# A second group of cached keys from the turned layout in every step, and a head's loads moved to other slots

## The chip, the cores and the metric

One core of a Trainium2 chip. The metric is the device time of one execution in microseconds, the median of three runs. All arithmetic is float32.

## What is computed

Two layers of a decoder for 1024 prompt tokens and, beside them, 8 samples of 8 new tokens each. Layer 0 has a gated linear recurrence (HGRN2, 4 heads) and latent attention (MLA, 4 heads) side by side, layer 1 another recurrence; each is followed by an MLP. The change concerns layer 0, and there the attention of the 64 new tokens to their samples' caches, 64 pages of 128 rows each:

```
past = cache_mla[e][page_table].reshape(Bd, past_len, LAT_DIM)      # 8 x 8192 rows of 320
s = (einsum('bqhc,bkc->bhqk', q_lat, c_kv) + einsum('bqhr,bkr->bhqk', q_pe, k_pe)) * MLA_SCALE
p = softmax(where(k_pos <= q_pos, s, NEG_BIG))
out = einsum('bhqk,bkc->bqhc', p, c_kv)                             # c_kv: the first 256 of 320
```

The recurrence is evaluated in chunks, per head: with log decays summed along the tokens, the pairs within a chunk are formed level by level (distance 1, 2, 4 ... 64), each level a product of decayed queries and keys.

## The kernel before

The program is a row of stages with a barrier between them: load, even (layer 0's projections), latent, prompt attention, **mix**, even out, MLP, then layer 1. Stage mix (`even_mix_stage`) does the cached attention of the samples and, in its gaps, the recurrence of the 4 heads.

**Attention.** 512 pages are worked off in 32 steps of 16 pages; a step is 4 groups of 4 pages, and a sample is 4 steps. POOL fetches the rows of a group with one indirect DMA (`ask_for_rows`) into a ring of 12 slots, after the values of two steps before have been formed (`pool.wait_ge(valued, step)`). For the scores a key must lie turned, 128 features on the partitions. It comes so in one of two ways. Either PE transposes the rows it has (`turn_keys`, L2229), four 128x128 pieces to a unit, through the four PSUM banks KB, from which ACT or DVE copies each unit into `keys` (L2408, L2587: DVE takes units 1 and 3). Or SP loads the pages from a copy of the cache that the host has turned (`ask_for_keys`, L1660: for each page read its number from the table into a register, and issue a DMA of 160 KB). A group of the second kind needs only its 256 value columns from POOL (L1649) instead of all 320 (L1651). Group 3 (`M.COME`) is of the second kind in every step, with two buffers `kd`. Group 2 is so in the even steps from 2 on (`M.TWICE`), with one buffer `kd_more`; in the others it is transposed:

```
def units(step):
    return 5 if step in M.TWICE else 8
```

Units 0 to 4 are the keys of groups 0 and 1 (20 transposes), units 5 to 7 those of group 2 (10 transposes, and 512, 512 and 256 columns to copy, all by ACT).

**Order on PE.** Written out by hand. `score` waits for the copies of the step's keys and for both kinds of loaded keys (L2236, L2238).

```
for step in range(STEPS):
    score(step)
    slot(2 * step)
    turn_p(step - 1)                      # if step
    turn_keys(step + 1, 0), turn_keys(step + 1, 1)
    value(step - 1)                       # if step
    turn_keys(step + 1, 2 ...)
    slot(2 * step + 1)
```

**Head work.** There are two slots per step. A head h takes 16 of them; its own slot at slot n is n + 4 - 16 h, so that heads overlap by a few slots. On PE own slot 5 transposes the values, 3 or 6 to 13 hold the levels (`level`, L2302, each waits for `a_out`: DVE's `keep` of the level before), 15 the output (L2324 to L2333), 17 the head's end (L2341, L2348). `value` waits, at a head's own slot 4, for the first `keep` (L2272). On DVE a step is slot(2 step), `maxima`, the copy of unit 1, `gather`, the copy of unit 3, slot(2 step + 1); `keep` (L2676 to L2688) stands in the slots, and own slot 19 (3 of the next head) forms a head's last product (`apply_gate`, L2729).

**SP's queue** issues, in order, for each step: slot(2 step), the keys of step + 2 after the score of the step (`fetch_keys`), slot(2 step + 1). In a head's own slots: 1 store the last head's sample states and, when that has landed, load the next (`next_state`); 2 load the next head's decay gate (`next_gate`, after `b_made`), then wait for the last product `final`, store it, and load the values (`next_value`); 5 the output gate; 12 the next queries; 14 the prompt state.

Of the kernel before, what the change touches and what calls it, by code (L numbers as in the profile page):

```python
# [19 lines left out]
I32 = mybir.dt.int32  # L20
# [1111 lines left out]
def even_stage(nc, K, M, following):  # L1132
# [16 lines left out]
    with Stage(nc, "even") as s:  # L1149
# [18 lines left out]
        following_in, const_in, weight_in = (s.sem(n) for n in ("following_in", "const_in", "weight_in"))  # L1168
# [13 lines left out]
        def _(sp):  # L1182
# [15 lines left out]
            for g in range(2, N + 2):  # L1198
                if g < N:
                    sp.wait_ge(lo_done, g - 1)  # L1200
                    load(g)
                if g == 4:
                    for dst, src in ((M.cos, K.c_cos), (M.sin, K.c_sin), (M.rot, K.c_rot), (M.diag, K.c_causal)):
                        sp.dma_start(dst[:], src).then_inc(const_in, 16)
                    sp.dma_start(M.w_uq[:], K.w_uq[0].rearrange("(k p) (h n) -> p k h n", p=P, h=HEADS)).then_inc(const_in, 16)
                    sp.dma_start(M.wuk[:], K.w_uk[0].rearrange("h (k p) n -> p (h k) n", p=P)).then_inc(const_in, 16)
                    for k in range(2):
                        sp.dma_start(M.wuv[:, k, :, :], K.w_uv[0][:, k * P:(k + 1) * P, :].rearrange("h p v -> p h v")
                                     ).then_inc(const_in, 16)
                if g == N:  # L1210
                    sp.wait_ge(lo_done, (N + 1) // 2 * 2 - 1)
                    load_following(sp, K, following, following_in)
                store(g - 2)
            sp.wait_ge(const_in, 16 * 8)
            sp.wait_ge(following_in, 16)
# [438 lines left out]
def ask_for_keys(sp, K, M, pages, step):  # L1654
# [8 lines left out]
    if step in M.TWICE:  # L1663
        ask(M.COME - 1, M.kd_more, M.kd_more_in)


def prompt_attention_stage(nc, K, M):
# [15 lines left out]
    with Stage(nc, "pattn") as s:  # L1683
# [16 lines left out]
        rows_out = s.sem("rows_out")  # L1700
# [7 lines left out]
        def _(sp):  # L1708
            sp.dma_start(pages[:], K.page_table.broadcast_to([P, NB * PAGES])).then_inc(table_in, 16)
            sp.dma_start(unit[:], K.c_unit).then_inc(table_in, 16)  # L1710
            sp.dma_start(K.xT[:, 7, :], K.c_starts).then_inc(starts_in, 16)
            sp.dma_start(K.rows_prompt.rearrange("(i p) c -> p i c", p=P), M.rows[:]).then_inc(rows_out, 16)
            sp.dma_start(K.rows_sample, M.rows_new[:]).then_inc(rows_out, 16)
# [6 lines left out]
            sp.wait_ge(rows_out, 32)  # L1720
# [20 lines left out]
        def _(dve):  # L1741
# [26 lines left out]
            def running_sum():  # L1768
# [4 lines left out]
                dve.tensor_tensor_scan(K.xT[:, M.HB, :], K.xT[:, 7, :], logf, 0.0, ALU.mult, ALU.add)  # L1773
# [105 lines left out]
def even_mix_stage(nc, K, M):  # L1879
# [73 lines left out]
    with Stage(nc, "mix") as s:  # L1953
        lat = s.sb("lat", [P, RING - M.AHEAD, ROWF])
# [22 lines left out]
        levels, starts, own = s.sb("levels", [P, L, P], I32), K.acc, s.sb("own", [NS, NB])  # L1977
        M.kd_more, M.kd_more_in = s.sb("kd_more", [P, 4, LAT]), s.sem("kd_more_in")
# [21 lines left out]
        cleared = s.sem("cleared")  # L2000
# [23 lines left out]
        def ring_slot(i):  # L2024
            return M.lat[:, i, :] if i < M.AHEAD else lat[:, i - M.AHEAD, :]
# [28 lines left out]
        def _(sp):  # L2054
# [12 lines left out]
            def next_state(h):  # L2067
                store_s0(h - 1)
# [26 lines left out]
            def slot(n):  # L2095
                for h in range(HEADS):
                    own_slot = n + LEAD - SLOTS * h
                    if own_slot == 1 and h:
                        next_state(h)
                    if own_slot == 2 and h + 1 < HEADS:  # L2100
                        next_gate(h)
                    if own_slot == 2 and h:
                        next_value(h)
                    if own_slot == 5:
                        output_gate(h)
                    if own_slot == 12 and h + 1 < HEADS:
                        next_query(h)
# [4 lines left out]
            sp.dma_start(starts[:], K.c_starts).then_inc(h_const, 16)  # L2112
            sp.dma_start(levels[:], K.c_levels).then_inc(h_const, 16)
            sp.dma_start(own[:], K.c_own).then_inc(h_const, 16)
# [4 lines left out]
            sp.dma_start(s0[:], K.state_hgrn[0][:, 0, :, :].rearrange("b k v -> k b v")).then_inc(s0_in, 16)  # L2119
# [3 lines left out]
            for step in range(STEPS):  # L2123
# [3 lines left out]
                slot(2 * step + 1)  # L2127
            sp.wait_ge(x_made, 7 * HEADS)
# [13 lines left out]
            sp.wait_ge(row_back, 16 * (2 * HEADS - 1))  # L2142

        @block.gpsimd
        def _(pool):
# [55 lines left out]
            pool.wait_ge(h_const, 48)  # L2201
# [11 lines left out]
        def _(pe):  # L2213
# [18 lines left out]
            def score(step):  # L2232
# [4 lines left out]
                if step in M.TWICE:  # L2237
                    pe.wait_ge(M.kd_more_in, 64 * (M.TWICE.index(step) + 1))  # L2238
                if step:
                    pe.wait_ge(expd, step)  # L2240
                for f, part_of in enumerate(FORMS):
                    odd, c = f // 3, f % 3
                    for j in range(GR):
                        out = S[j * Q:(j + 1) * Q, odd * 256:(odd + 1) * 256]
                        if j in turned_groups(M, step):
                            col = c * P + (odd * 64 if c < 2 else 0)
                            turned_in = (kd[:, step % 2] if j == M.COME else M.kd_more)[:, :, col:col + 64]
# [333 lines left out]
        def _(dve):  # L2581
# [203 lines left out]
            dve.wait_ge(h_const, 48)  # L2785
# [1379 lines left out]
def first_mixers(nc, K, between, following):  # L4165

    with ExitStack() as stack:
# [8 lines left out]
        M.AHEAD, M.COME, M.TWICE = 4, 3, tuple(step for step in range(NB * PAGES // 16) if step % 2 == 0 and step)  # L4176
# [3 lines left out]
        with ExitStack() as prompt:  # L4180
# [3 lines left out]
            even_stage(nc, K, M, between)  # L4184
# [10 lines left out]
        even_mix_stage(nc, K, M)  # L4195
# [151 lines left out]
```

## Time and profile before

| | us |
|---|---|
| median of 3 runs | 3021.35 (3016.34 to 3023.03) |
| the profiled execution | 3019.65 |
| its span, first to last instruction | 3017.8 |
| busy in the span: PE, weight loads, DVE, ACT, POOL | 2916.4, 2700.0, 1605.9, 1210.8, 1638.0 |
| TensorE clock granted, mean | 0.988 of full speed |
| bytes moved by DMA | 472 MB, 156 GB/s |

How the rows below are read. All times are us from the start of the span. A **timeline** row gives the start, the time from there to the end of the last of its instructions, the engine ("q": its queue, here SP's DMA issues), line, operation, out<-in by the program's names, the shape, how many, and in brackets how long the engine had stood idle before and what ended that. A **wait** row gives total us, times and the longest. A row by **stretch** gives each engine's busy us and number of instructions, the granted clock, and the DMA engines' busy share and GB/s. A **group** row gives shapes, number, busy us, mean ns of one, and the idle time before them. A **DMA issue** row gives how many, KB each where known, and the median us from issue to landing.

### The profile page before, as it was taken

What the parts mean: (1) busy time and instruction counts of PE and PEld (TensorE: products, weight loads), DVE (VectorE), ACT (ScalarE), POOL (GpSimd) and SP (SyncE); (2) the same over time, 40 slices, a digit from 0 to 9 for tenths busy, and PEclk for the clock granted to TensorE, in tenths of its full rate; (3) what the DMA queues carried; (4) which work ended last, traced back from release to release, by engine and by line L of the source; (5) the groups of instructions that cost most, each with busy time, mean ns of one, the idle gap of its engine ahead of it and who ended that gap; (6) DMA issues with size and microseconds to landing.
All of it is one profiled execution on the core that took longest, in us unless ns stands there. A gap on an engine that the chain in (4) does not pass through costs nothing. (4 is left out here: it accounts for less than half of the span.)

```text
span 3017.8 us, 55813 instructions
## 1 busy us (share of the span) xinstructions
PE 2916.4 (97%) x22247; PEld 2700.0 (89%) x22247; DVE 1605.9 (53%) x2214; ACT 1210.8 (40%) x2106; POOL 1638.0 (54%) x1372
## 2 busy tenths in 40 slices
PE   8999999999999999999999999999999999999998
PEld 8998666676678999998999989998899999989998
DVE  3222365556553564457666627724546554476665
ACT  4211435545552434434444442313534344344443
POOL 1122103555531167788999615721111787799995
PEclk9999999999999999999999999999999999999999
DMA  5122206888873144446434134658532344454442
GB/s 192 36 88 80 86 15 223 286 284 312 293 264 109 43 146 134 151 131 224 147 140 146 66 117 154 228 211 299 191 118 62 126 154 139 151 207 138 146 139 81
DMA packets 324994, 472.09 MB, mean 156 GB/s; under 512 B 21537, under 2 KB 222689, under 8 KB 324610
## 3 DMA queue, kind: packets, MB, share of 16 engines
q1 hardware_dynamic: 304002, 383.77, 38.0%
q0 software_dynamic: 19872, 82.46, 7.6%
q8 instruction: 178, 2.92, 0.4%
q10 hardware_dynamic: 864, 2.31, 0.2%
q14 instruction: 78, 0.64, 0.1%
HBM read 343.11 MB, written 125.35 MB: 155 GB/s over the span
## 5 line engine op out<-in xcount | busy, mean ns | idle before, releaser
L112 PE MATMUL mlp_X<-mlp_f_hi,mlp_w_hi 128*128 128x272 f32 x1968 | 568.6, 289 | 9.4 <-DVE xT L934 7.6
L113 PE MATMUL mlp_X<-mlp_f_lo,mlp_w_hi 128*128 128x272 f32 x1968 | 568.0, 289 | 0.0
L114 PE MATMUL mlp_X<-mlp_f_hi,mlp_w_lo 128*128 128x272 f32 x1968 | 567.1, 288 | 0.0
L769 POOL TENSOR_TENSOR mlp_w_lo<-mlp_raw,mlp_w_hi 128x256 fp32r<-128x256 f32 (+1 forms) x348 | 346.2, 1002 | 156.0 <-ACT mlp_w_hi L653 114.3
L112 PEld LDWEIGHTS mlp_X<-mlp_f_hi,mlp_w_hi 128*128 128x128 f32 x1968 | 370.4, 188 | 12.0 <-DVE xT L934 9.1
L113 PEld LDWEIGHTS mlp_X<-mlp_f_lo,mlp_w_hi 128*128 128x128 f32 x1968 | 371.0, 189 | 0.0
L114 PEld LDWEIGHTS mlp_X<-mlp_f_hi,mlp_w_lo 128*128 128x128 f32 x1968 | 370.7, 188 | 0.0
L769 POOL TENSOR_TENSOR mlp_w_lo<-mlp_sums,mlp_w_hi 128x256 fp32r<-128x256 f32 (+1 forms) x276 | 309.7, 1122 | 13.4 <-ACT mlp_w_hi L653 9.9
L112 PE MATMUL mlp_Z<-mlp_f_hi,mlp_w_hi 128*128 128x272 f32 x976 | 281.5, 288 | 2.7 <-DVE xT L934 1.3
L113 PE MATMUL mlp_Z<-mlp_f_lo,mlp_w_hi 128*128 128x272 f32 x976 | 281.7, 289 | 0.0
L114 PE MATMUL mlp_Z<-mlp_f_hi,mlp_w_lo 128*128 128x272 f32 x976 | 281.2, 288 | 0.0
L934 DVE TENSOR_TENSOR xT<-xT,mlp_X 128x544 f32<-128x544 f32 x256 | 184.0, 719 | 131.2 <-PE mlp_X L114 129.1
L653 ACT ACTIVATE mlp_w_hi<-mlp_sums 128x256 fp32r<-128x256 f32 (+1 forms) x276 | 127.6, 478 | 309.8 <-POOL mlp_sums L769 267.0
L653 ACT ACTIVATE mlp_w_hi<-mlp_raw 128x256 fp32r<-128x256 f32 (+1 forms) x340 | 157.8, 466 | 128.9 <-PE mlp_X L114 99.2
L112 PEld LDWEIGHTS mlp_Z<-mlp_f_hi,mlp_w_hi 128*128 128x128 f32 x976 | 183.7, 188 | 3.7 <-DVE xT L934 1.8
L113 PEld LDWEIGHTS mlp_Z<-mlp_f_lo,mlp_w_hi 128*128 128x128 f32 x976 | 184.0, 189 | 0.0
L114 PEld LDWEIGHTS mlp_Z<-mlp_f_hi,mlp_w_lo 128*128 128x128 f32 x976 | 183.8, 188 | 0.0
L112 PE MATMUL odd_bank<-odd_x_hi,odd_w_hi 128*128 128x352 f32 (+1 forms) x552 | 180.9, 328 | 0.0
L114 PE MATMUL odd_bank<-odd_x_hi,odd_w_lo 128*128 128x352 f32 (+1 forms) x552 | 180.4, 327 | 0.0
L113 PE MATMUL odd_bank<-odd_x_lo,odd_w_hi 128*128 128x352 f32 (+1 forms) x552 | 180.2, 326 | 0.0
L112 PE MATMUL even_bank<-even_x_hi,even_w_hi 128*128 128x352 f32 (+1 forms) x504 | 165.4, 328 | 0.0
L114 PE MATMUL even_bank<-even_x_hi,even_w_lo 128*128 128x352 f32 (+1 forms) x504 | 164.7, 327 | 0.0
(579 smaller groups left out, 7579.5 us busy)
## 6 DMA issues: line engine op xcount, KB each, us to landing
hidden<-mlp_ev SPq DMA_DIRECT2D x224, 272.0 KB, 2.3
mlp_f_lo_plain<-hidden SPq DMA_DIRECT2D x112, 544.0 KB, 5.5
mlp_raw<-in_w_down SPq DMA_DIRECT2D x64, 512.0 KB, 3.5
mlp_raw<-in_w_up SPq DMA_DIRECT2D x48, 512.0 KB, 5.7
mla_kd<-in_cache_turned SPq DMA_DIRECT2D x128, 160.0 KB
projections<-odd_zout SPq DMA_DIRECT2D x24, 544.0 KB, 4.2
forms<-gla_f SPq DMA_DIRECT2D x20, 544.0 KB, 2.7
mix_kd_more<-in_cache_turned SPq DMA_DIRECT2D x60, 160.0 KB, 6.5
```

Of the source, the lines that this page charges most:

```text
L112: pe.matmul(out, w_hi, x_hi, start=first, stop=False, skip_group_check=onto)
L113: pe.matmul(out, w_hi, x_lo, start=False, stop=False, skip_group_check=onto)
L114: return pe.matmul(out, w_lo, x_hi, start=False, stop=last, skip_group_check=onto)
L653: act.activation(slot(i)[0], src, ACT.Copy).then_inc(whi_done, 1)
L769: pool.tensor_tensor(to, x, y, op).then_inc(done_by, 1)
L934: dve.tensor_tensor(dst, dst, read_x(bank), ALU.add).then_inc(added, 1)
```

## The change

- `M.TWICE` holds every step from 2 on: group 2's keys come turned in the odd steps from 3 on too. `kd_more` and its semaphore are doubled, by the step's parity.
- Ring slots that only ever hold values (group 3's) shrink from 320 to 256 columns a row; the table of levels moves to the persistent buffer `K.first`. It and the starts (into `K.acc`) are loaded in the prompt attention stage.
- `K.first` held the first weights of the stage after mix, loaded in the even stage. They are loaded near the end of mix now, after the last level is kept (`a_out`).
- SP's own slots: 2 wait for `final`, load the values, then store the product; 4 store the sample states; 6 load the next ones (head 0's too, which was at the stage's start); 8 the output gate; 10 the next decay gate; 12 and 14 as before.

```diff
-        ask(M.COME - 1, M.kd_more, M.kd_more_in)
+        ask(M.COME - 1, M.kd_more[:, step % 2], M.kd_more_in[step % 2])
...
+        M.levels = K.first[:].bitcast(I32).rearrange("p (l t) -> p l t", l=len(LEVELS) + 1)
...
-            sp.dma_start(K.xT[:, 7, :], K.c_starts).then_inc(starts_in, 16)
+            sp.dma_start(K.acc[:], K.c_starts).then_inc(starts_in, 16)
...
             for step in range(2):
                 ask_for_keys(sp, K, M, pages, step)
+            sp.dma_start(M.levels, K.c_levels).then_inc(ends, 16)
...
-        lat = s.sb("lat", [P, RING - M.AHEAD, ROWF])
+        lat = [s.sb(f"lat{i}", [P, BL * KV_LORA if i % GR == M.COME else ROWF]) for i in range(M.AHEAD, RING)]
...
             def next_state(h):
-                store_s0(h - 1)
                 sp.wait_ge(s0_stored, 16 * h)
                 sp.dma_start(s0[:], K.state_hgrn[0][:, h, :, :].rearrange("b k v -> k b v")).then_inc(s0_in, 16)
...
             def next_value(h):
+                sp.wait_ge(final, h)
+                sp.dma_start(vg[:], K.z[row(Z_I, h), :]).then_inc(v_in, 16)
                 store_o(h - 1)
-                sp.dma_start(vg[:], K.z[row(Z_I, h), :]).then_inc(v_in, 16)
...
-                    if own_slot == 1 and h:
-                        next_state(h)
-                    if own_slot == 2 and h + 1 < HEADS:
-                        next_gate(h)
                     if own_slot == 2 and h:
                         next_value(h)
-                    if own_slot == 5:
+                    if own_slot == 4 and h:
+                        store_s0(h - 1)
+                    if own_slot == 6:
+                        next_state(h)
+                    if own_slot == 8:
                         output_gate(h)
+                    if own_slot == 10 and h + 1 < HEADS:
+                        next_gate(h)
...
+            sp.wait_ge(a_out, L * HEADS)
+            load_following(sp, K, following, following_in)
...
                 if step in M.TWICE:
-                    pe.wait_ge(M.kd_more_in, 64 * (M.TWICE.index(step) + 1))
+                    pe.wait_ge(M.kd_more_in[step % 2], 64 * (M.TWICE.index(step) // 2 + 1))
...
-        M.AHEAD, M.COME, M.TWICE = 4, 3, tuple(step for step in range(NB * PAGES // 16) if step % 2 == 0 and step)
+        M.AHEAD, M.COME, M.TWICE = 4, 3, tuple(step for step in range(NB * PAGES // 16) if step >= 2)
```

## Rows read from the trace of the kernel before

**Rows 1.** Stage mix: us, then PE, PEld, DVE, ACT, POOL, clock, DMA

```profile
478.00:906.00 428.00, 399.51 (x4458) 294.01 (x4458) 252.50 (x435) 228.85 (x442) 219.02 (x168) 0.97 0.84 291
```

**Rows 2.** What PE waited for, 545 to 906 us: total, times, longest

```profile
PE mix_KB L2229 <- DMA mix_lat<-in_cache_mla,mla_index: 8.9, 5, 2.7
PE mix_KB L2229 <- DMA mla_lat<-in_cache_mla,mla_index: 3.4, 3, 1.7
PE mix_KB L2286 <- DMA mix_vg<-projections: 2.1, 1, 2.1
```

**Rows 3.** Timeline of PE, 621 to 662 us (steps 10 to 12)

```profile
624.94 2.62 PE L2229 MATMUL mix_KB<-ident,mix_lat 128*128 128x128 f32 x22
628.19 2.02 PE L2302 MATMUL mix_HB<-xT 128*128 128x128 f32 x16 [0.62 <-DVE mix_a L2688]
639.42 1.53 PE L2229 MATMUL mix_KB<-ident,mla_lat 128*128 128x128 f32 x12
655.34 2.02 PE L2302 MATMUL mix_HB<-xT 128*128 128x128 f32 x16
```

**Rows 4.** Timeline of DVE, 621 to 662 us

```profile
627.78 0.26 DVE L2688 COPY_PREDICATED mix_a<-mix_levels,mix_O 64x32 f32<-64x32 int32 x1
654.45 0.74 DVE L2683 COPY_PREDICATED mix_a<-mix_levels,mix_HB 128x512 f32<-128x512 int32 x1
```

**Rows 5.** Timeline of POOL: the second ask of step 14

```profile
680.20 0.95 POOL L1651 DMA_INDIRECT mix_lat<-in_cache_mla,mla_index  x1 [0.30 <-issue]
```

**Rows 6.** POOL DMA issue at 680 us, landing last

```profile
mix_lat<-in_cache_mla,mla_index POOLq DMA_INDIRECT x1, 7.8
```

**Rows 7.** Timeline of PE where a head starts (steps 9, 17, 25)

```profile
604.27 0.65 PE L2252 MATMUL mix_S<-mix_keys,mix_q 128*32 128x256 f32 x3 [0.95 <-ACT mix_v_tok L2477]
688.55 1.04 PE L2229 MATMUL mix_KB<-ident,mix_lat 128*128 128x128 f32 x8
700.87 1.07 PE L2229 MATMUL mix_KB<-ident,mix_lat 128*128 128x128 f32 x8 [2.60 <-DMA mix_lat<-in_cache_mla,mla_index]
702.07 3.46 PE L2276 MATMUL mix_O<-mla_lat,mix_pT 128*32 128x256 f32 x32
710.18 0.42 PE L2252 MATMUL mix_S<-mix_keys,mix_q 128*32 128x256 f32 x3 [0.81 <-DMA mla_kd<-in_cache_turned]
714.96 1.06 PE L2229 MATMUL mix_KB<-ident,mla_lat 128*128 128x128 f32 x8 [1.39 <-DMA mla_lat<-in_cache_mla,mla_index]
815.14 0.42 PE L2252 MATMUL mix_S<-mix_keys,mix_q 128*32 128x256 f32 x3
820.79 1.06 PE L2229 MATMUL mix_KB<-ident,mix_lat 128*128 128x128 f32 x8 [2.26 <-DMA mix_lat<-in_cache_mla,mla_index]
```

**Rows 8.** Timeline of DVE, 696 and 701 us: last product, first kept level

```profile
696.21 1.27 DVE L2729 TENSOR_TENSOR xT<-xT,mix_vg 128x1088 f32<-128x1088 f32 x1
701.72 0.21 DVE L2678 COPY_PREDICATED mix_a<-mix_levels,mix_O 64x64 f32<-64x64 int32 x1
```

**Rows 9.** Timeline of SP where a head starts

```profile
592.64 8.57 SPq L1660 DMA_DIRECT2D mla_kd<-in_cache_turned  x8
697.89 0.44 SPq L2079 DMA_DIRECT2D mix_vg<-projections  x1
699.43 8.25 SPq L1660 DMA_DIRECT2D mla_kd<-in_cache_turned  x8
805.97 8.16 SPq L1660 DMA_DIRECT2D mla_kd<-in_cache_turned  x8
```

**Rows 10.** SP DMA issues at 602, 624, 836 us, landing last

```profile
mix_kd_more<-in_cache_turned SPq DMA_DIRECT2D x4, 160.0 KB, 8.0
mix_kd_more<-in_cache_turned SPq DMA_DIRECT2D x4, 160.0 KB, 5.2
mix_kd_more<-in_cache_turned SPq DMA_DIRECT2D x4, 160.0 KB, 2.8
```

**Rows 11.** Stretch behind step 9 pauses, columns as rows 1

```profile
603.40:610.10 6.70, 5.83 (x51) 3.03 (x52) 4.23 (x4) 3.13 (x7) 3.38 (x2) 0.50 1.02 393
```

More of the change, by code:

```diff
@@ L1167, in even_stage @@
         M.z_stored = [16 * len(STORED[i::2]) for i in range(2)]
-        following_in, const_in, weight_in = (s.sem(n) for n in ("following_in", "const_in", "weight_in"))
+        const_in, weight_in = s.sem("const_in"), s.sem("weight_in")
         lat_squared, lat_added, lat_mean, lat_logged, lat_rstd, lat_normed = (s.sem(n) for n in (
@@ L1710, in _ @@
             sp.dma_start(unit[:], K.c_unit).then_inc(table_in, 16)
-            sp.dma_start(K.xT[:, 7, :], K.c_starts).then_inc(starts_in, 16)
-            sp.dma_start(K.rows_prompt.rearrange("(i p) c -> p i c", p=P), M.rows[:]).then_inc(rows_out, 16)
-            sp.dma_start(K.rows_sample, M.rows_new[:]).then_inc(rows_out, 16)
+            sp.dma_start(K.acc[:], K.c_starts).then_inc(starts_in, 16)
+            sp.dma_start(K.rows_prompt.rearrange("(i p) c -> p i c", p=P), M.rows[:]).then_inc(ends, 16)
+            sp.dma_start(K.rows_sample, M.rows_new[:]).then_inc(ends, 16)
             sp.wait_ge(table_in, 32)
@@ L1719, in _ @@
                 sp.dma_start(K.mix[512 + h * P:512 + (h + 1) * P, 0:SEQ], o[:, h % 2, :]).then_inc(stored[h % 2], 16)
-            sp.wait_ge(rows_out, 32)
+            sp.wait_ge(ends, 48)
         @block.gpsimd
@@ L1772, in running_sum @@
                 dve.wait_ge(clamped, 1)
-                dve.tensor_tensor_scan(K.xT[:, M.HB, :], K.xT[:, 7, :], logf, 0.0, ALU.mult, ALU.add)
+                dve.tensor_tensor_scan(K.xT[:, M.HB, :], K.acc[:], logf, 0.0, ALU.mult, ALU.add)
             soften(0)
@@ L1976, in even_mix_stage @@
         pages = nc.alloc_sbuf_tensor_at("mix_pages", [P, NB * P], I32, offset=nc.sbuf_base - 4 * NB * P)[NS:NS + 1, 0:NB * PAGES]
-        levels, starts, own = s.sb("levels", [P, L, P], I32), K.acc, s.sb("own", [NS, NB])
-        M.kd_more, M.kd_more_in = s.sb("kd_more", [P, 4, LAT]), s.sem("kd_more_in")
+        levels, starts, own = M.levels, K.acc, s.sb("own", [NS, NB])
+        M.kd_more, M.kd_more_in = s.sb("kd_more", [P, 2, 4, LAT]), [s.sem("kd_more_in0"), s.sem("kd_more_in1")]
         last_dec = s.sb("last_dec", [P, C + NB])
@@ L2024, in ring_slot @@
         def ring_slot(i):
-            return M.lat[:, i, :] if i < M.AHEAD else lat[:, i - M.AHEAD, :]
+            return M.lat[:, i, :] if i < M.AHEAD else lat[i - M.AHEAD][:]
         def latents(step, j):
@@ L2118, in _ @@
             sp.dma_start(pages, K.page_table).then_inc(table_in, 16)
-            sp.dma_start(s0[:], K.state_hgrn[0][:, 0, :, :].rearrange("b k v -> k b v")).then_inc(s0_in, 16)
+            sp.dma_start(own[:], K.c_own).then_inc(h_const, 16)
             sp.wait_ge(table_in, 16)
@@ L2142, in _ @@
             sp.wait_ge(row_back, 16 * (2 * HEADS - 1))
+            sp.wait_ge(following_in, 16)
         @block.gpsimd
@@ L2246, in score @@
                             col = c * P + (odd * 64 if c < 2 else 0)
-                            turned_in = (kd[:, step % 2] if j == M.COME else M.kd_more)[:, :, col:col + 64]
+                            turned_in = (kd if j == M.COME else M.kd_more)[:, step % 2, :, col:col + 64]
                             end = pe.matmul(out.rearrange("q (r g u) -> q r g u", r=2, u=32), q[:, 6 if f == 5 else c, b, :],
@@ L4183, in first_mixers @@
             M.cos, M.sin, M.rot = (keep(prompt, n, [P, w]) for n, w in (("cos", T), ("sin", T), ("rot", P)))
-            even_stage(nc, K, M, between)
+            even_stage(nc, K, M)
             M.ckv, M.kpe = K.xT[:, 3:5, :], K.xT[:, 5, :]
@@ L4194, in first_mixers @@
         M.pn, M.m_new, M.den_new = keep(stack, "pn", [Q, NB, NS]), keep(stack, "m_new", [Q, NB]), keep(stack, "den_new", [Q, NB])
-        even_mix_stage(nc, K, M)
+        even_mix_stage(nc, K, M, between)
         even_out_stage(nc, K, M, following)
```

19 lines of the change are left out of this document (6 added, 13 removed).

## The prediction

> **What bounds the kernel now.** Read first the busy time by stretch: the stage "mix", in which the cached attention and the head work run side by side, takes 428 of the 3018 us, PE is busy for 399.5 of them, DVE for 252.5, ACT for 228.9, POOL for 219.0, and the DMA engines for 84% [rows 1]. The change touches this stage and little else. PE is the bound on average, but the DMA has little idle time to lend. Then read what PE waits for, over most of the stage: rows from the cache, eight times and 12.3 us (8.9 and 3.4), and once 2.1 us for the head's values [rows 2]. A total says nothing of what a shorter PE is worth: for that, read step by step what starts right after the transposes that the change removes. I number the steps 0 to 31; a head's work takes eight of them, so that each place comes back every eight steps.
>
> **What is removed.** Each odd step from 3 on, 15 in all, loses units 5 to 7: ten transposes and three ACT copies. The keys of the others take 1.53 us for the last twelve transposes of a step (639.42), those of an odd step 2.62 us for the last twenty-two (624.94) [rows 3], so ten are worth 1.09 us, 16.4 us in all if nothing took their place. The score has as many matmuls as before, with another source. The copies fall on ACT, which is busy for 229 of 428 us [rows 1]; I take them as nothing, PE covers them. Without that cover, where ACT is late at a head's end, their going only lets PE keep its own 1.09.
>
> **Where it goes, eight steps.** PE turns the keys of a step while it works on the step before, and the saved stretch lies ahead of that step's second slot of head work. While the keys of steps 3 and 5 (and each eighth from there) are turned, that slot holds a level, which waits until DVE has kept the level before. DVE does that behind its copy of unit 3, which PE feeds at the same moment as before. At steps 3, 11, 19, 27: DVE ends at 628.04 (627.78 + 0.26) [rows 4], PE goes on at 628.19, having already waited 0.62 us [rows 3]. Without ten transposes it waits 1.71. At steps 5, 13, 21, 29: DVE ends at 655.19 (654.45 + 0.74) [rows 4], PE's level starts at 655.34, right behind the transposes with no gap shown, just the 0.15 us after DVE that the other place has [rows 3, 4]. Here it waits 1.09 instead. So eight of fifteen give nothing.
>
> **Four steps that give something.** Behind the transposes for 7, 15, 23 and 31 comes a head's end, no DVE result is due, and PE moves ahead by 1.09 us. It then meets the rows of the next step: POOL's second ask, issued at 680.20, landed 7.8 us later [rows 5, 6], at 688.0, and the transposes began at 688.55 [rows 7]. I take 0.5 us for the first three and the full 1.1 us for the last, which has no step behind it.
>
> **The three steps at a head's start, 9, 17 and 25.** Their keys are asked for late. SP stands in the wait for the previous head's last product before it, in this step and in this one only: DVE ends that product at 697.48 (696.21 + 1.27) [rows 8], SP then issues the values at 697.89 and the first key ask at 699.43 [rows 9]. The store, the values and the keys behind them stay there; the change swaps the first two and moves the state's, gate's and decay's loads to later slots. But now eight asks go out instead of four. Eight of them take 8.25 us with the last one's own 0.34 in it, 1.1 us from one to the next [rows 9], and the last of step 17 goes out at 699.43 + 7.7 = 707.1, less the 0.5 us gained before: 706.6. How long it takes to land has three rows: 2.8 us where the queues are light, 5.2 where a burst of cache rows falls in, 8.0 at a head's start with all its loads [rows 10]. Since those loads are moved away and the burst is not, I take 5.2 and keep 2.8 and 8.0 for the range. Then:
> - step 17: score at 711.8, where it stood at 710.18. Late by 1.6. The 1.39 us wait for rows at 714.96 is covered by this [rows 7]: +0.2. PE would be ready at 710.18 less the 0.81 it waited for keys less 1.6 of gains, 707.8, and stands for 4.0 us. What such a pause may do is in the clock row: behind the pauses of step 9 PE ran at 0.50 of its clock, its lower level of 1.2 GHz, for 6.7 us, which costs half of them, 3.4 [rows 11]. I add half of that, 1.7, for one more stretch: +1.9.
> - step 9: 592.64 + 7.7 - 0.5 + 5.2 = 605.0 against 604.27 [rows 7, 9]: +0.7. The wait for values goes, and is inside the new one; the slow clock stays.
> - step 25: 805.97 + 7.7 - 0.5 + 5.2 = 818.4 against 815.14, late by 3.3, less the 2.26 us wait for rows behind it, which is covered [rows 7, 9]: +1.0. Here too a slow stretch stays.
>
> The waits for rows ahead of these steps (2.60 us ahead of step 17) give nothing back when they shrink: the values behind them start at 702.07, 0.14 us after DVE has kept the head's first level (701.72 + 0.21) [rows 7, 8], and would wait for that instead.
>
> A rule speaks against this reading. The Trainium skill ("DMA: Bandwidth & Descriptors", Issuing engines are not separate DMA queues) holds that the sequencer time to initiate a DMA is usually small relative to the DMA itself. By it eight asks would cost next to nothing more than four, and the three steps would start earlier than before, as in the first rival. The rows disagree for 160 KB asks whose page number is first read from a table: 1.1 us each [rows 9].
>
> **Traffic.** A group whose keys come turned fetches only values, 131 KB less, and 655 KB of keys more: 0.52 MB in each odd step, 7.9 MB on the stage's some 125 MB (291 GB/s over 428 us [rows 1]). The eight waits for rows sum to 12.3 us; the five at heads' starts take 2.7, 1.7 (the longest of each row), 2.60, 2.26 and 1.39, so three others take 1.6 [rows 2, 7]. These three are all in even steps, whose rows travel beside eight key asks; odd steps get eight asks now. I give three of them the same 0.5 us each: +1.6; ends 0 and 5.
>
> **At nothing.** The table of levels and the starts go to the stage before, covered by its PE work; uncovered they would cost one landing, at most 8.0 [rows 10]. The weights of the next stage are loaded from step 29 on, two steps of 13.4 us (428 over 32) ahead of need; late, they too would cost one landing. The moved store, state, gate and decay loads put an issue of 0.34 us each ahead of an ask at other steps, on SP alone. There a step's eight asks take 8.9 us and the last lands within 8.0, 17 us of the two steps, 27 us, that lie between the first ask and its score: 10 us cover them. The state's load waits for a store two slots old, with keys behind it, inside the same 10 us.
>
> **Sum.** +0.7 + 1.9 + 1.0 + 1.6 - 1.1 = +4.1 us against the profiled execution's 3019.65, which lies 1.7 below the median of the runs: 3025 us after. A measurement of this kernel tells about 0.2% (6 us) from no change, so this is a forecast of no change.
>
> **Rivals.**
> - *Keys in time: faster.* If the last ask lands by the time PE is ready, the waits at heads' starts only shrink. PE would be ready at 9 by 4.7 us earlier (2.1 for values, 0.95 for ACT, 1.6 of gains) [rows 2, 7] without the slow stretch (3.4); at 17 by 2.4 and the row wait of 1.39, at 25 by 1.6 and 2.26, with one slow stretch less (1.7); and 1.1 at the end: 18.6 in all, with the traffic 17 us faster, 3004. For it: the head's loads do bunch there, and a landing of 2.8 exists [rows 10]. Against: even so step 17's last ask lands at 709.4, and PE is ready at 707.8. Part of it can come, all hardly: 0.27 for over 6 us of it.
> - *The jam stays: slower.* If the last ask takes 8.0 us, each of the three is 2.8 later, 8.4 in all; pauses of up to 8 us bring another slow stretch at two of them, 3.4; and late rows at their upper end add 3.4: +19.3 in all, 3041. The point from which it decides is a landing above some 6 us. For it: last asks with a row burst beside them run longer than the median of four. Against: 1.6 MB less in the queue there (state stored and loaded, 512 KB each, gate 544). 0.33, half measures included.
> - *DVE places cost the clock.* The eight places now pause for 1.1 to 1.7 us, less than the pauses behind which the clock fell at step 9. If two of eight fall badly: +3.4; inside the range.
> - *No change*, by the sum: 0.40.
>
> For the range, the first rival is reached to two thirds and the second to three quarters: 3010 to 3037.
>
> **What would show it.** Right: transposes of the cached keys fall from 810 to 660; PE's waits for levels kept by DVE grow by 8.7 us (eight times 1.09); a wait of PE's score for the second key buffer or the first at 9, 17, 25 of 3 to 6 us, and SP's eight asks at 1.1 us; the wait for values gone. Wrong: if steps 3 and 5 and their kin are over 0.5 us shorter, the DVE reading is false; if no score waits for keys, the first rival holds; if scores wait for keys at steps other than 9, 17 and 25, SP can't keep eight asks a step and the result is slower than I say.

## The result, and the profile after

| | before | after |
|---|---|---|
| median of 11 runs each, us | 3021.92 (3016.34 to 3031.12) | 3037.91 (3032.05 to 3045.45) |
| ratio of the medians, 95% interval | | 1.0046 (1.0036 to 1.0057) |
| the profiled execution, us | 3019.65 | 3045.45 |
| its granted TensorE clock, mean | 0.988 | 0.986 |

The change makes the kernel 16 us slower; the prediction said 3025 us and no change. The profiled execution after is 7.5 us above its own median and the one before 2.3 below, so the two traces lie 26 us apart where the medians lie 16 apart. 3038 us lies just above the forecast's range of 3010 to 3037. The same kernel, run again with the last experiment, was 11 us slower than the kernel before on that chip; its trace, called the second trace, is used beside this one.

The stage first: the stretch of [rows 1] in the kernel after (same columns).

```profile
478.00:906.00 428.00, 365.04 (x4031) 265.70 (x4031) 242.80 (x412) 194.53 (x371) 215.63 (x165) 0.94 0.85 290
```

PE is busy for 365 us of 428 where it was for 399.5, and its clock is 0.94, not 0.97. Only part of that is work removed: the kernel after is some 29 us behind by the end of this stretch, so less of its stage falls inside. Over the whole kernel PE has 150 matmuls fewer (22247 before, 22097 after) and is busy for 2903.6 us in place of 2916.4 (2896.9 in the second trace). What it waits for, from 545 to 930 us of the kernel after (total, times, longest), answers to [rows 2]:

```profile
PE mix_S L2252 <- DMA mix_kd_more<-in_cache_turned: 26.0, 3, 10.6
PE mix_HB L2302 <- DVE mix_a L2683: 7.0, 9, 1.1
PE mix_HB L2302 <- issue: 5.5, 4, 1.7
PE mix_O L2276 <- DVE mix_a L2678: 4.8, 3, 1.7
...
PE mix_KB L2229 <- DMA mix_lat<-in_cache_mla,mla_index: 2.3, 3, 1.3
PE mix_HB L2302 <- DVE mix_a L2688: 1.7, 1, 1.7
PE mix_KB L2229 <- DMA mla_lat<-in_cache_mla,mla_index: 1.4, 2, 0.9
```

The rows of the cache, 12.3 us before, are down to 3.7 (7.4 in the second trace), and the wait for a head's values is gone. In their place three scores wait 26 us for the second buffer of turned keys (18.5 in the second trace). These are the starts of steps 9, 17 and 25, as the timeline of PE has them:

```profile
618.07 0.64 PE L2252 MATMUL mix_S<-mix_keys,mix_q 128*32 128x256 f32 x2 [9.20 <-DMA mix_kd_more<-in_cache_turned]
...
731.51 0.64 PE L2252 MATMUL mix_S<-mix_keys,mix_q 128*32 128x256 f32 x2 [10.56 <-DMA mix_kd_more<-in_cache_turned]
...
843.35 0.64 PE L2252 MATMUL mix_S<-mix_keys,mix_q 128*32 128x256 f32 x2 [6.21 <-DMA mix_kd_more<-in_cache_turned]
```

And SP's timeline ahead of two of them (steps 9 and 17), which answers to [rows 9]:

```profile
599.96 0.33 SPq L2076 DMA_DIRECT2D mix_vg<-projections  x1
600.34 0.43 SPq L2063 DMA_DIRECT2D mixed<-xT  x1
601.52 4.11 SPq L1656 DMA_DIRECT2D mla_kd<-in_cache_turned  x4
606.40 3.80 SPq L1656 DMA_DIRECT2D mix_kd_more<-in_cache_turned  x4
...
711.97 0.33 SPq L2076 DMA_DIRECT2D mix_vg<-projections  x1
712.34 0.43 SPq L2063 DMA_DIRECT2D mixed<-xT  x1
713.53 4.13 SPq L1656 DMA_DIRECT2D mla_kd<-in_cache_turned  x4
718.43 4.08 SPq L1656 DMA_DIRECT2D mix_kd_more<-in_cache_turned  x4
```

Values, store, then eight asks. The last ask's 0.34 us begin at 609.86, 722.17 and (step 25, four asks from 832.85 for 3.60) 836.11, so the scores come 8.2, 9.3 and 7.2 us behind it. SP's next issue behind the last ask is the 512 KB store of the last head's sample states, at 610.20, 722.55 and 836.49: moved from own slot 1 to own slot 4, it still goes out right behind them. During the last four asks of step 17 the DMA engines have hardly an idle slice and move more than the 290 GB/s of the stage; the view of the DMA for 718 to 722.4 us:

```profile
DMA packets 883, 1.62 MB, mean 368 GB/s; under 512 B 105, under 2 KB 686, under 8 KB 882
```

Step by step, from the starts of the scores in both traces, the block from step 8 to 10 is longer by 4.3 us, 16 to 18 by 7.2, and 24 to 26 by 3.1 (3.9, 2.4 and 2.4 in the second trace). The stretches between two scores in which the keys of 3, 11, 19 and 27 are turned differ from before by 0.0 us in the second trace, those with the keys of 5, 13, 21 and 29 by 0.0 too (here 0.2 to 0.3 longer): no gain there, as forecast. In this trace three of the first four, from the scores of steps 10, 18 and 26, are 1.4 us longer, and not by the clock, which is 1.00:

```profile
629.90:646.30 16.40, 13.91 (x155) 10.47 (x155) 9.69 (x16) 4.85 (x11) 10.70 (x9) 1.00 0.97 360
```

```profile
632.55 0.39 PE L2248 MATMUL mix_S<-mix_kd_more,mix_q 128*32 128x256 f32 x1 [0.68 <-issue]
```

The score of step 10 stops inside, with nothing shown that it waits for, and takes 4.1 us in place of 2.8. The second trace of the same kernel has no such stop, those of most experiments have it; its cause is open. One more piece is new, 6.2 us between the first two scores of the stage (1.7 in the second trace).

### The profile page after: what moved, and what is told of

It reads as the page before. It is cut to its first block and busy times, and to the rows that moved or that the text cites. A ratio compares the mean times of both kernels' runs of the same rounds, so it can differ in the third digit from the quotient of the medians.

```text
span 3043.7 us, 55776 instructions
## 1 busy us (share of the span) xinstructions
PE 2903.6 (95%) x22097; PEld 2684.6 (88%) x22097; DVE 1606.2 (53%) x2214; ACT 1191.9 (39%) x2061; POOL 1638.6 (54%) x1372
```

## The experiments

All are edits of the changed kernel. SP's key asks and the wait that holds them were tried first, four kernels on one chip, where the kernel before took 3023.21 us.

**Four asks instead of eight, at three steps.** Steps 9, 17 and 25 leave out the second turned group and turn its keys on PE again, as before.

```diff
-tuple(step for step in range(NB * PAGES // 16) if step >= 2)
+tuple(step for step in range(NB * PAGES // 16) if step >= 2 and step not in (9, 17, 25))
```

> The changed kernel, but steps 9, 17 and 25 transpose group 2's keys again (12 odd steps turned instead of 15). Theory A, SP asks for eight pages too late behind the previous head's last product: the three waits for the second key buffer (26.0 us in the changed kernel's trace) are gone, the waits for the first buffer stay under 1 us each, and the kernel is some 15 us faster than the changed one: about 3022. Theory B, the traffic of 7.9 MB more is what costs: only a fifth of it goes, 3 us faster, 3035. Theory C, the lost time is at the stage's start, where DVE's small operation ran 4.6 us beside POOL's differences (6.2 us between the first two scores): nothing of that changes, and the kernel is as slow as before this edit but for what A gives.

Measured: 3021.96 us (3016.67 to 3029.66), 0.9995 of before (0.9981 to 1.0010), by the ratios 15 us below the change. All of the loss is in three steps of thirty. The waits for the second buffer are gone. Two scores, of steps 9 and 25, still wait for the first, longer than the 1 us each that was expected (545 to 930 us):

```profile
PE mix_S L2252 <- DMA mla_kd<-in_cache_turned: 5.5, 2, 3.8
```

**Eight asks, ahead of the wait.** All 15 steps keep the second turned group. In steps 7, 15 and 23 SP asks for the keys first, and then stands in the wait for the last product with the values and the store behind it.

```diff
-                slot(2 * step)
+                late = any(2 * step + LEAD - SLOTS * h == 2 for h in range(1, HEADS))
+                if not late:
+                    slot(2 * step)
                 if step + 2 < STEPS:
                     fetch_keys(step + 2)
+                if late:
+                    slot(2 * step)
```

> The changed kernel, but in the three steps in which SP stands in the wait for a head's last product, it asks for the eight pages of keys before that wait. All 15 odd steps stay turned and the bytes are the same. Theory A: the waits for the second key buffer at steps 9, 17, 25 go, and the time falls by 15 us or more, to 3015 to 3023. Theory B (traffic): the time stays within 4 us of the changed kernel's 3038, since not a byte less is moved.

Measured: 3018.73 us (3013.37 to 3028.27), 0.9986 (0.9971 to 1.0002), by the ratios 18 us below the change, with not a byte less moved than in the change. SP's timeline for the keys of step 9 (lines have moved by four in this kernel):

```profile
590.71 3.63 SPq L1656 DMA_DIRECT2D mix_kd_more<-in_cache_turned  x4
594.47 0.41 SPq L2076 DMA_DIRECT2D mix_vg<-projections  x1
```

The second buffer's asks are out before the values. No score waits for keys any more, and the next wait in size is the rows again (545 to 930 us):

```profile
PE mix_KB L2233 <- DMA mix_lat<-in_cache_mla,mla_index: 9.7, 6, 2.0
PE mix_HB L2306 <- DVE mix_a L2687: 7.9, 10, 1.1
...
PE mix_KB L2233 <- DMA mla_lat<-in_cache_mla,mla_index: 2.0, 1, 2.0
```

So eight asks of 1.1 us are no loss by themselves; eight asks that can't start before the last product are.

**The start of the stage.** POOL's first difference of the stage is held behind DVE's first difference of the keys, against the 6.2 us between the first two scores.

```diff
                 if n == 0:
+                    if h == 0:
+                        pool.wait_ge(k_diff, 1)
```

> The changed kernel, but POOL's first difference waits until DVE has formed the distances to the chunk ends, as it happened to lie in the kernel before. Theory C, DVE and POOL hold each other up at the stage's start because the shorter start lets POOL begin 2.4 us sooner: DVE's small operation takes 0.2 us again instead of 4.6, the first two scores lie 7 to 8 us apart instead of 13.6, and the kernel is 5 to 6 us faster: 3032. Rival: the long DVE operation was an accident of one execution, or the lost time returns in the next wait: no difference, 3038.

Measured: 3038.3 us (3032.32 to 3042.83), 1.0050 (1.0036 to 1.0064): the time of the change. The first two scores are 7.7 us apart in its trace, 7.3 before, so the stretch at the start is repaired and still nothing is won in the median, where 5 to 6 us were expected.

**The moves without the group.** Second turned group in even steps only, all loads and buffers moved as changed.

```diff
-tuple(step for step in range(NB * PAGES // 16) if step >= 2)
+tuple(step for step in range(NB * PAGES // 16) if step >= 2 and step % 2 == 0)
```

> The changed kernel's order of loads and its memory, but group 2 turned in the even steps only, as before. It isolates the moved loads. Theory A: no wait for keys at steps 9, 17, 25 over 1 us, the wait for values (2.1 us) gone, the rows' waits at the heads' starts smaller: 3 to 10 us faster than the kernel before, if theory C's 6 us at the start were not there; with them, within 4 us of 3022. Rival: the moved loads themselves cost (keys asked late behind them): some 3030 with waits for keys elsewhere.

Measured: 3023.34 us (3020.74 to 3029.03), 1.0004 (0.9991 to 1.0017). Within the interval, 4 us to each side, the moves cost and bring nothing.

The next four, on another chip where the kernel before took 3029.22 us, ask why the repaired kernel gains so little: they cross the second group of the odd steps (with, without) with DVE's order (late, early). **The control** is the kernel with keys first, with POOL held too.

> The change with the keys asked for ahead of the wait for the last product in steps 7, 15 and 23 (as in the kernel with keys first), and POOL's first difference of the stage held behind the first difference of the keys. It is the control for the next one. The kernel that held POOL back alone had the time of the change (1.005 of before against 1.0046), so both theories expect the time of the kernel with keys first: 0.9986 of the kernel before, 3018 to 3019 us, no wait of a score for the second key buffer, and PE's waits for levels that DVE kept as in the changed kernel, some 12 us in all.

Measured: 3021.18 us (3016.52 to 3028.77), 0.9967 (0.9950 to 0.9985).

**DVE keeps the level first.** In the odd slots DVE's kept level stands ahead of its copy of unit 3:

```diff
-                    if own_slot == (4 if h else 7):
+                    if own_slot == (4 if h else 7) and not (n >= 0 and own_slot % 2):
                         keep(h, 0)
-                    if 8 <= own_slot <= 14:
+                    if 8 <= own_slot <= 14 and not (n >= 0 and own_slot % 2):
                         keep(h, own_slot - 7)
...
+                for h in range(HEADS):
+                    own_slot = 2 * step + 1 + LEAD - SLOTS * h
+                    if own_slot == 7 and not h:
+                        keep(h, 0)
+                    if own_slot in (9, 11, 13):
+                        keep(h, own_slot - 7)
                 if later:
                     copy_keys(step + 1, 3)
```

> The control with one thing more: in the odd slots DVE keeps the level of the head work before its copy of unit 3, not behind it. Theory: at the keys of steps 3, 5 and each eighth from there the change gives nothing because PE waits for that kept level; then the waits on DVE's kept levels fall from some 12 us to under 4, the blocks that turn those keys become 1.1 us (steps 3 and kin 1.7 us) shorter, and the whole 8 to 11 us, 3007 to 3011 us. Rival: something else releases PE there at the same moment (rows of the next step, ACT's results, DVE's copy itself, which now comes later and holds back the score), the waits only change their name, and the time stays at the control's within 2 us.

Measured: 3014.5 us (3010.95 to 3017.41, six runs), 0.9945 (0.9923 to 0.9966), 6.7 us below the control; this version beats both kernels. PE's waits in the control, and then in this kernel (545 to 930 us, both):

```profile
PE mix_HB L2308 <- DVE mix_a L2689: 8.1, 10, 1.1
...
PE mix_HB L2308 <- issue: 3.4, 2, 1.7
...
PE mix_HB L2308 <- DVE mix_a L2694: 1.7, 1, 1.7
```

```profile
PE mix_KB L2235 <- DMA mix_lat<-in_cache_mla,mla_index: 10.9, 6, 2.7
PE mix_KB L2235 <- DMA mla_lat<-in_cache_mla,mla_index: 3.8, 3, 1.7
...
PE mix_S L2254 <- issue: 2.6, 7, 1.0
PE mix_HB L2308 <- issue: 2.2, 4, 0.7
...
PE mix_HB L2308 <- DVE mix_a L2689: 1.4, 3, 0.6
```

The level's matmuls waited 13.2 us and wait 3.6 now. (The two traces lie 13.7 us apart, the medians 6.7: the control's traced execution is 6.9 above its median.) From score to score, against the control: the four stretches with the keys of steps 3, 11, 19 and 27 are 0.8, 1.0, 1.0 and 1.0 us shorter (1.7 expected); those with the keys of 5, 13, 21 and 29 by 0.0, 0.0, 0.1 and 0.8 (1.1 expected), because the score at the start of three of them now stops inside: at steps 4, 12 and 20 it takes 3.5 to 3.7 us, not 2.8, and the level behind it waits 0.1 to 0.4 us longer. The score's waits for DVE's copies stand ahead of its first matmul, and the trace shows nothing that the stop waits for; whether the later copy has a part in it is not shown. The stretches behind these four, from the scores of 5, 13, 21 and 29, are 1.8, 0.4, 1.0 and 1.5 us longer. And five stretches of which I had not thought, from the scores of steps 1, 3, 11, 19 and 27, are 1.0 to 1.25 us shorter each. The gain is less than the 8 to 11 us expected, more than the rival's 2.

**The same two without the odd steps' group.** First the control, then the early keeping.

> The control with the second turned group only in the even steps, as before the change: the loads spread, the keys asked for first, POOL held back. The difference to the control is what the second group of the odd steps is worth once its keys are in time. Theory (eight of fifteen places give nothing, the others up to 1.09 us each, some of it given back to late rows): the control is 3 to 7 us faster, this kernel at 3021 to 3024 us. Rival (all fifteen places count): the control is 12 to 16 us faster, which would need this kernel at 3031 or more. Rival (the traffic takes all back): no difference.

Measured: 3026.19 us (3023.01 to 3031.43), 0.9990 (0.9977 to 1.0003).

> As the one before, with DVE's early keeping too. Theory: with 22 transposes ahead of it PE comes to the kept level when DVE is nearly done (it waited 0.62 us at steps 3 and kin and nothing at 5 and kin), so keeping early gives at most 4 x 0.62 = 2.5 us here, against 8 to 11 us with the second group in the odd steps: 3019 to 3022 us. Then the odd steps' second group is worth 10 to 14 us with the early keeping and 3 to 7 us without. Rival: early keeping gives the same in both, so it is a gain of its own and not what hid the change's.

Measured: 3022.93 us (3015.75 to 3027.34), 0.9973 (0.9961 to 0.9986).

| medians, us | group in even steps | in all steps | worth of the odd steps' group |
|---|---|---|---|
| DVE keeps late | 3026.2 | 3021.2 | 5.0 |
| DVE keeps early | 3022.9 | 3014.5 | 8.4 |

With the keys in time, the second group of the odd steps is worth 5.0 us of the 16.4 that the removed transposes take, inside the 3 to 7 expected; with DVE keeping early it is worth 8.4, less than the 10 to 14 expected. Keeping early adds 3.3 us without the group (2.5 at most was expected) and 6.7 with it (8 at least was). Both sizes miss, and so do the two times themselves, 3021 to 3024 and 3019 to 3022 us expected. The traces say in part why: the five stretches of 1.0 to 1.25 us, 5.4 in all, come in both kernels, so this part of the early keeping is a gain of its own, as the rival had it; the four with the keys of 3, 11, 19 and 27 give 3.9 us with the group and 2.1 without. The intervals, 0.13% to 0.22% to each side, don't separate 3.3 from 6.7 firmly.

**What the spreading is worth, and the change once more.** On a third chip, the kernel before at 3017.55 us: SP's slots and their order put back as they were, beside the change itself.

```diff
-                sp.wait_ge(final, h)
+                store_o(h - 1)
                 sp.dma_start(vg[:], K.z[row(Z_I, h), :]).then_inc(v_in, 16)
-                store_o(h - 1)
...
+                    if own_slot == 1:
+                        if h:
+                            store_s0(h - 1)
+                        next_state(h)
+                    if own_slot == 2 and h + 1 < HEADS:
+                        next_gate(h)
                     if own_slot == 2 and h:
                         next_value(h)
-                    if own_slot == 4 and h:
-                        store_s0(h - 1)
-                    if own_slot == 6:
-                        next_state(h)
-                    if own_slot == 8:
+                    if own_slot == 5:
                         output_gate(h)
-                    if own_slot == 10 and h + 1 < HEADS:
-                        next_gate(h)
```

> The change with SP's loads and stores of a head at their old slots and in their old order (state stored and loaded at slot 1, gate and values at slot 2, the output's store ahead of the values, the decays at slot 5), everything else as changed: it tells what the spreading is worth beside the second group. Theory (the last of eight late key asks lands in 7 to 9 us because the queues are full at a head's start, and the spreading keeps 1.6 MB of the head's loads out of them): the landings of steps 9, 17 and 25 grow by up to 5 us each (1.6 MB at 291 GB/s is 5.5 us), the three waits for the second key buffer sum to 30 to 40 us instead of 26, and the whole is 5 to 15 us slower than the change. Rival (what fills the queues is the key asks and the rows of the cache themselves, not the head's loads; its issues of 0.34 us each are all that it adds on SP): within 3 us of the change.

> The change itself once more, beside the one before on the same chip, as its control and for a second trace of it: 1.0046 of the kernel before as measured first. If the 4.6 us operation of DVE at the start of the stage was an accident of one execution, this trace has it at 0.2 us, and the first two steps of the stage start 7.4 to 8.7 us apart; if it belongs to the change, it stands there again and the first block is 6 us longer.

Measured: old slots 3035.63 us (3034.22 to 3038.48), 1.0057 (1.0044 to 1.0071); the change again 3028.69 (3027.53 to 3030.53), 1.0036 (1.0023 to 1.0050). The spreading is worth 7 us beside the second group. From the start of the last ask to the score the old slots take 10.4, 11.1 and 7.2 us, the change here 8.1, 5.5 and 5.8. The three waits sum to 22.3 us against 18.5, and 4.3 us of waits for values come back: less than the 30 to 40 us expected. The clock differs too. Windows of the same three stretches, with the columns of [rows 1], for the kernel before, the change again, the old slots and keys first:

```profile
600.00:635.00 35.00, 31.32 (x345) 22.56 (x345) 23.43 (x32) 18.56 (x39) 19.94 (x16) 0.90 0.94 332
700.00:735.00 35.00, 31.17 (x343) 23.53 (x343) 25.77 (x39) 17.79 (x37) 21.08 (x18) 0.95 0.97 358
805.00:845.00 40.00, 35.26 (x376) 25.44 (x380) 27.46 (x41) 19.46 (x42) 23.56 (x18) 0.91 0.92 325
```

```profile
600.00:635.00 35.00, 25.69 (x297) 18.37 (x297) 21.19 (x33) 13.34 (x27) 17.14 (x13) 0.85 0.96 343
700.00:735.00 35.00, 27.80 (x314) 19.39 (x313) 25.22 (x32) 14.62 (x29) 21.45 (x16) 0.90 0.97 332
805.00:845.00 40.00, 32.18 (x347) 22.21 (x340) 27.85 (x36) 15.86 (x31) 22.43 (x17) 0.87 0.93 309
```

```profile
600.00:635.00 35.00, 24.80 (x263) 17.81 (x264) 18.17 (x27) 12.41 (x26) 17.44 (x13) 0.80 0.86 307
700.00:735.00 35.00, 22.59 (x235) 15.12 (x231) 17.68 (x28) 12.99 (x24) 15.62 (x13) 0.76 0.85 306
805.00:845.00 40.00, 29.32 (x328) 20.16 (x331) 25.63 (x37) 15.28 (x30) 19.41 (x15) 0.87 0.88 307
```

```profile
600.00:635.00 35.00, 30.13 (x336) 21.44 (x332) 22.36 (x35) 16.04 (x34) 21.88 (x17) 0.99 1.01 361
700.00:735.00 35.00, 29.39 (x302) 19.92 (x303) 23.18 (x35) 14.13 (x28) 18.68 (x14) 0.90 1.00 346
805.00:845.00 40.00, 33.12 (x355) 23.18 (x348) 28.09 (x41) 16.89 (x33) 24.37 (x20) 0.96 1.02 360
```

The figure behind the busy times is the clock, an average over stretches at 2.4 GHz (1.0) and 1.2 GHz (0.5). Length times (1 - clock) is what a PE that is busy throughout would lose: over the three stretches 8.9 us before, 14.0 with the change, 20.6 with the old slots, and 5.5 with the keys first. But a PE that stands and waits loses nothing by a low clock, and much of the growth is of that kind. In the first trace of the change, each pause and the piece of work behind it:

```profile
608.87:618.07 9.20, 0.00 (x1) 0.03 (x1) 5.17 (x4) 4.52 (x8) 6.46 (x5) 0.70 1.01 361
618.07:625.00 6.93, 6.93 (x68) 4.08 (x72) 1.29 (x4) 1.08 (x2) 0.00 (x0) 0.66 0.93 285
720.95:731.51 10.56, 0.00 (x0) 0.03 (x1) 5.11 (x4) 4.44 (x8) 6.41 (x4) 0.70 1.03 369
731.51:738.00 6.49, 6.49 (x68) 3.92 (x72) 1.25 (x4) 1.08 (x2) 0.00 (x0) 0.70 0.64 192
837.14:843.35 6.21, 0.01 (x1) 0.03 (x1) 5.07 (x4) 4.28 (x8) 4.47 (x4) 0.83 1.02 355
843.35:850.00 6.65, 6.65 (x64) 3.87 (x68) 1.13 (x5) 1.18 (x3) 2.00 (x1) 0.64 0.98 352
```

The clock fell inside the pauses. Behind them the busy PE lost 2.4, 1.9 and 2.4 us, and behind the pauses of 9.0, 4.5 and 5.1 us of the second trace 2.1, 1.7 and 2.9: a longer pause did not bring a longer slow stretch of work. In the kernel before, waits of only 2.1 and 0.95 us stand at step 9, and the low clock there cost 3.4 us [rows 11].

## Where the prediction was right and where it was wrong

The runs of one chip list a mean clock for each execution. The same product over the whole kernel, averaged over the runs:

| kernel | median less before, us | at the low clock, less before, us | the rest, us |
|---|---|---|---|
| the change (again) | +11.1 | 36.3 - 26.8 = +9.5 | +1.6 |
| with POOL held | +15.1 | 40.2 - 26.9 = +13.3 | +1.8 |
| old slots | +18.1 | 42.5 - 26.8 = +15.7 | +2.4 |
| four asks at three steps | -1.2 | 30.8 - 26.9 = +3.9 | -5.1 |
| keys first | -4.5 | 26.6 - 26.9 = -0.3 | -4.2 |

This is bookkeeping with an upper bound, and it does not say that the clock cost 9.5 us: the pauses are in the middle column too. In the traces the bound is far from the cost. From score 8 to 11, 16 to 19 and 24 to 27 together the product is 8.5 us before, 15.1 and 13.7 in the two traces of the change; 0.5, 7.0 and 3.5 of it lie in pauses at these scores, and 8.0, 8.1 and 10.2 are left for a busy PE.

- **Ten transposes of 1.09 us, 16.4 us: right.** The transposes of cached keys fall by 150 (in the lines of 478 to 936 us from 530 + 280 to 430 + 230); over the whole kernel PE's busy time falls by 12.8 and 19.5 us in the two traces.
- **Eight places give nothing: right in the time.** The waits of the level's matmuls grow from 5.0 us (3.1 + 1.9) to 14.2 (7.0 + 5.5 + 1.7), by 9.2 where 8.7 was said (by 7.6 in the second trace), the longest 1.71 us as worked out. That DVE's order alone holds them is shown for half of them: with the level kept first, the keys of 3, 11, 19 and 27 give up to 1.0 us, those of 5, 13, 21 and 29 next to nothing, although the wait of 1.07 us is gone there: the stop inside the score takes it.
- **Four steps that give something: right in size in the second trace.** The block from step 30 is 1.22 us shorter in the second trace (1.1 said). Those from 6, 14 and 22 are shorter by 1.2, 1.4 and 2.9, and 0.0, 1.4 and 1.6 us come back one step later, the last two with new waits for rows of 1.25 and 1.43 us: 2.4 us are kept where 1.5 were said. In the first trace only 0.8 are kept, and the last block is 0.5 longer.
- **Where the jam is, and what SP does in it: right.** The place (9, 17, 25), the wait for the last product ahead of it and 1.1 us an ask came as said: 8.3 us from the first ask to the end of the last at step 17 of the second trace (706.90 to 715.17), 8.25 before. The Trainium skill ("DMA: Bandwidth & Descriptors", Issuing engines are not separate DMA queues) has the time to initiate a DMA as usually small beside the DMA; by that the three waits would not be there. The traces disagree for these asks, and the waits for the second buffer went only when its asks were left out or moved ahead of the wait.
- **"I take 5.2": the step that failed.** The last ask was to land in 5.2 us, between 2.8 and 8.0. From its start to the score it took 8.2, 9.3 and 7.2 us in one trace and 8.1, 5.5 and 5.8 in the other, 7.4 on average, and three of the six lay above the upper bound. I argued that the head's loads had left this stretch. The spreading is worth 7 us, but the store of 512 KB had not left, and the change itself puts four asks of 160 KB there, 655 KB more, into queues that moved 368 GB/s while they were issued. Three landings, 2.2 us longer each, are 6.6 us. Trace by trace it accounts for nearly all that these places lack: the three blocks were to grow by 5.1 us (0.7 + 1.9 + 1.0 and the 1.5 gained ahead of them), the late landings make it 5.1 + 9.2 in the first trace and 5.1 + 3.8 in the second, and the blocks grew by 14.6 and 8.7. How much of a late landing is owed to the asks themselves, to the store and to the rows of the cache beside them is not separated by any run.
- **"I add half of that, 1.7, for one more stretch": about right in the traces.** The busy PE lost 0.1 and 2.2 us more than before in these blocks. Two errors cancelled there: the pauses took 4.5 to 10.6 us, not 3 to 6, and the slow stretch of work behind them was not longer for it. By the table up to 9.5 us are possible over the whole kernel; the traced execution of before had more low clock (0.988) than the runs of before in the table (0.991 on average), so the traces don't rule out a larger share. That part stays open.
- **Traffic, +1.6: not shown.** Rows that were late at a head's start are covered by the new wait, as said. But the 1.4 and 1.6 us above are given back where PE came early, which the half gains of those steps had counted already, and the stretches of the second trace that no other term names sum to -0.3 us. What DVE keeps at a head's start is late next in the place of rows, 4.8 us where it was 1.0.
- **Moved loads at nothing: right in time**, by the kernel that has them alone (1.0004). At the stage's start the cover was not what I thought: see the last section.

With 7.4 us for the landing the sum is 4.1 + 6.6 = +10.7 us, against +16 and +11 measured. By the second trace, where the three landings are 3.8 us longer than forecast, it is +7.9, and that trace is 8.0 us longer than the one of the kernel before. So close a match is part luck: the sum has 1.6 us of traffic that the trace hasn't, and lacks the 1.7 us at the stage's start. What the first has beyond it, 6.2 us at the stage's start and three stops of 1.4 us inside scores, was in no term. This is the second rival's mechanism, whose deciding point, a landing above some 6 us, was met in four of six places; I gave it a third of the chance. The choice between ends far apart went to a middle row that had only four asks behind it. That the time came out at the edge of the range is owed to its width, not to the middle value.

## What to carry to other kernels

If a queue issues in order and one of its entries waits for the end of a phase, count what stands behind it each time work is added to that queue: here the same second group made the kernel 16 us slower with its asks behind the wait, and no slower than before with them ahead of it (0.9986, and 0.9967 in the control), by moving one call. Price a landing from a row with as much in the queue as the new plan will put there, not from the median of lighter ones, and price the slow clock of a pause by the busy time that it covers (some 2 to 3 us behind each pause of 4.5 to 10.6 us here), not by the length of the low clock, most of which may fall into the pause itself. When a removed stretch gives nothing, look at what the next instruction waits for on another engine, and at what it would wait for next: reordering two DVE instructions gave 6.7 us, but not all in the places that had asked for it.

## What the runs showed of the hardware

An instruction of DVE stood beside POOL's tensor operations. From the timelines of DVE and POOL, first the kernel after, then the change again:

```profile
491.93 4.62 DVE L2782 TENSOR_SCALAR mix_nm_new<-mla_m_new 32x8 f32<-32x8 f32 x1
...
492.56 3.97 POOL L2170 TENSOR_TENSOR mix_dec<-xT 128x1088 f32<-128x1088 f32 x2
```

```profile
493.87 5.77 DVE L2637 TENSOR_TENSOR xT<-xT 128x1024 f32<-128x1024 f32 x2
...
494.45 3.96 POOL L2170 TENSOR_TENSOR mix_dec<-xT 128x1088 f32<-128x1088 f32 x2
```

Before the change the first took 0.16 us and the second 1.36, and both were over when POOL began at 493.00. Now POOL no longer waits for the starts and the levels, begins within 0.7 us of DVE's instruction, and DVE is done only when POOL is, at 496.5, or 1.2 us later. The Trainium skill ("SBUF — State Buffer", SBUF: two separate sides) describes a port pair that DVE and POOL share, locked for a whole instruction, so that the other fully blocks. The second pair of rows fits, an operation with two inputs in SBUF; that a tiny operation with one input takes 4.62 us the rule doesn't explain: it began 0.63 us ahead of POOL and takes 0.16 alone, so by the rule it would have been over before. The kernel before has a smaller case beside the same POOL pair, which ends at 496.96:

```profile
495.39 1.61 DVE L2645 COPY mix_last_dec<-xT 128x8 f32<-128x8 f32 x1
496.92 0.16 DVE L2646 COPY mix_last_dec<-xT 128x8 f32<-128x8 f32 x1
```

So such a record is not new with the change. The same page of the Trainium skill counts operations in a 2-port perf mode among those that take the lock; whether the tiny ones ran in it no row shows. Operations with two inputs stand behind them in both cases, and no run here separates the two. Between the first two scores 6.2 us are lost in one trace and 1.7 in the other, and still the kernel that holds POOL back is no faster in the median: whatever the collision costs, the change's 16 us are not there. The kernel before had medians of 3017.6, 3023.2 and 3029.2 us on three chips, so kernels of one chip are compared here by their times, the rest by ratio.
